# An expert layer's weights loaded in 8 KB runs, with its down product in high and low parts

## The chip, the cores and the metric

The kernel runs on one core of one Trainium2 chip. The time is that of one execution on the device, in microseconds (us). The reference's outputs have to be met within the tolerance of the problem.

## What is computed

The input is one sequence of 512 tokens of width 1024 (and 256 context tokens). A first block of layers (modulation, two scans, attention-free mixing, a feed-forward layer) is followed by two layers of a second block. Each of these ends in a mixture of experts, and only that is touched here. Cut to it, for one layer:

```python
# 32 experts, 2 of them for each of 512 tokens; w_gate, w_up [32, 1024, 256]; w_down [32, 256, 1024]
def expert_block(args):
    xe, e = args
    hid = jax.nn.silu(xe @ w_gate[e]) * (xe @ w_up[e])
    return hid @ w_down[e]
yb = lax.map(expert_block, (xb, block_expert)).reshape(-1, d)
```

The rows that come out are weighted by the router's probabilities and added up for each token. All is float32. The weights of one expert are three matrices of 1 MB, 201 MB over 32 experts and two layers.

## The kernel before, in words

The program is written by hand for each engine: every engine has its own list of instructions, and semaphores order them. All weights of the whole kernel pass through a ring of four slots in SBUF, `ring` (L101), 16 KB per partition each. `load` (L220) is what SyncE (SP) does for one chunk: it waits until the slot is free (`chunk_free`, counted up by TensorE behind its last use) and issues two DMAs, both on the slot's own semaphore; `landed` (L225) waits for both. A second name, `ring_r`, gives the same memory as float32r.

A float32 product on TensorE runs as one slow fp32 matmul or, in `mm3` (L174), as three matmuls of float32r operands: each operand is parted into a high part (its value rounded by ScalarE in a Copy to float32r) and a low part (the difference, by VectorE), and high x high, high x low and low x high are added.

In a layer's expert stage, an expert b has two chunks (`ex_up`, `ex_down`, L2190): gate and up weights (2 MB) and down weights (1 MB). In SP's queue they stand as up(0), up(1), down(0), up(2), down(1) and so on, and in the ring each chunk takes the slot of the fourth before it. The loads of gate and up (`gu_halves`, L2197) put row k x 128 + p on partition p, side by side: each partition gets eight runs of 256 floats (1 KB) per matrix. The down load (`dn_halves`, L2201) takes rows f x 128 + p, f = 0 and 1, with one DMA for each f: 128 partitions, a run of 4 KB in each.

Every expert is given a block of 80 token rows. GpSimd gathers them (L2519) with an indirect DMA from `x_rows` in DRAM into `xg`, one row per partition on partitions 0 to 79. Then, for expert b in `body`:

- TensorE (L2307): gate and up product `up(b)`, 24 matmuls in two halves h over k (L2261, in `mm3`, recorded at L178 to L180); turning of the next expert's gathered rows, eight blocks of 128 columns (L2258); down product of expert b - 1 (L2271, 4 fp32 matmuls, 8 records at L154); turning of the hidden rows of b, two blocks (L2268). Behind `up` and `down` it frees the slot.
- ScalarE (L2402): high part of the next expert's gate and up weights, half 0 (L2357), waiting first for their landing and for the half buffer; silu of b (L2360); high part of the turned rows (L2354); half 1; copy of the turned hidden rows (L2363); issue of the store of the output rows of b - 1 to `y_rows` in DRAM (L2366), from partitions 0 to 79.
- VectorE (L2483): low parts of the two halves (L2441), in place in the ring, each behind its high part; between them the product of silu and up (L2444) and the low part of the turned rows (L2438); last, the copy of the output rows of b - 1 out of PSUM (L2447).

`first` and `last` are the same steps for the first and the last expert; `overflow` code runs only where an expert has over 80 rows. After the experts, GpSimd gathers each token's two rows back from `y_rows` (L2548, 128 partitions) and TensorE weights and adds them.

The high parts have one buffer for each half: half h of the next expert waits until TensorE is through with half h of this one:

```python
def w_hi(b, n, it, h, first=False):
    if h == 0:
        landed(act, ex_up(n), R + it)
    if not first:
        act.wait_ge(S(("ex_wu", "ex_gu")[h]), b)
    weights_hi(ex_up(n), h).then_inc(S("ex_wh"), 1)
```

Of the kernel before, what the change touches and what calls it, by code (L numbers as in the profile page):

```python
# [57 lines left out]
def build(nc, t):  # L58
    with ExitStack() as ctx:
# [38 lines left out]
        def large(suffix, dt, held):  # L98
            return [held.enter_context(nc.sbuf_tensor(n + suffix, shape, dt)) for n, shape in (
                ("hT", [P, KD, LAT + CTX]),  # L100
                ("ring", [P, SLOTS, KD, HB]),  # L101
                ("arena", [P, ARENA]))]

        with ExitStack() as place:
            hT, ring, arena = large("", F32, place)
        hT_r, ring_r, arena_r = large("_parts", F32R, ctx)
# [61 lines left out]
        def slot(n):  # L168
            return ring[:, n % SLOTS, :, :]
# [22 lines left out]
        def unit_of(chunks, n, q):  # L192

            return chunks[:, n % SLOTS, 2 * q:2 * q + 2, :].rearrange("p k (c n) -> p (k c) n", n=CTX)

        def slot_lo(n):
            return ring_r[:, n % SLOTS, :, :]
# [101 lines left out]
        lent = ring[:, LENT % SLOTS, :, :].rearrange("p k n -> p (k n)")  # L299
# [830 lines left out]
        def down_rows(n):  # L1130

            return ring[:, n % SLOTS, 0:4, :].rearrange("p (f h) n -> p f (h n)", f=2)
# [9 lines left out]
        def down_unit(chunks, k):  # L1142
            return chunks[:, (N_DN + k // 2) % SLOTS, 2 * (k % 2):2 * (k % 2) + 2, :].rearrange("p k (c n) -> p (k c) n", n=CTX)
# [1107 lines left out]
        def half_of(chunks, n, h):  # L2251

            return chunks[:, n % SLOTS, 4 * h:4 * h + 4, :]

        def experts_pe(pe, lay, R):
            def turn_rows(c):
                for k in range(KD):
                    last = nc.tensor.transpose(ps[:, k // 4, (k % 4) * CAP:(k % 4 + 1) * CAP], xg[:, c, k * P:(k + 1) * P], ident[0:CAP, 0:CAP])  # L2258
                return last

            def gate_up(c, n, h):  # L2261

                return mm3(ps[0:CAP, 2 + c, :], [(xt_hi[:, c, 4 * h + k, :], xt_lo[:, c, 4 * h + k, :], ew_hi[:, h, k, :], slot_lo(n)[:, 4 * h + k, :])
# [525 lines left out]
```

## Time and profile before

| what | us |
|---|---|
| median of 3 runs | 3377.92 |
| lowest and highest | 3375.75, 3384.12 |
| profiled execution, first to last instruction (span) | 3394.1 |
| expert stage of layer 1, about | 1840 to 2208 |
| expert stage of layer 2, about | 2984 to 3348 |

The profile was taken of one execution; for it the page gives the span, and no other time. Times in its views are us from the start of the span, unless marked ns. PE is TensorE, PEld its weight loads, DVE VectorE, ACT ScalarE, POOL GpSimd, SP SyncE. A digit in a row of 40 slices is the busy share of one slice of 84.9 us in tenths. The DMA share is that of 16 DMA engines; it can stand a little over 1, as packets of several queues overlap. Queue q1 carries SP's loads, q10 ScalarE's transfers, q0 GpSimd's gathers. In brackets behind a row of the timeline stands the idle time of the engine before it and what ended it.

### The profile page before, as it was taken

To read this page: it belongs to the slowest core of one execution; us is meant where nothing else is said; L and a number is where in the kernel's file an instruction comes from. 1 tells how busy PE (TensorE), PEld (TensorE's weight loads), DVE (VectorE), ACT (ScalarE), POOL (GpSimd) and SP (SyncE) were. 2 spreads that over 40 slices of the span, in tenths; PEclk is the share of its full clock that TensorE was granted. 3 is DMA by queue.
4 is the path that set the end of the run, shared out by engine and by line. 5 is a ranking of instruction groups with operands and counts; after the bars stand their busy time and mean duration, and the time that the engine had idled before them with its cause. 6 is when DMAs were issued, how large, how long until landed. Compare 5 with 4: busy or idle time off the path is not lost. (4 is left out here: it accounts for less than half of the span.)

```text
span 3394.1 us, 31106 instructions
## 1 busy us (share of the span) xinstructions
PE 2851.6 (84%) x10872; PEld 1823.9 (54%) x10872; DVE 1410.1 (42%) x2118; ACT 1094.6 (32%) x1661; POOL 176.3 (5%) x202
## 2 busy tenths in 40 slices
PE   7899876679998698789986988857968999688995
PEld 1464455367876475367774444425734777544442
DVE  0104177332223155333344555524543333465554
ACT  1103322132223346432222444314373222144441
POOL 0000000000000000000001111100000000021210
PEclk9889988889999799799996999978987999699998
DMA  8301200122223111022223999921201112289994
GB/s 308 117 25 50 96 1 7 48 75 81 68 75 115 51 50 50 0 87 75 75 89 107 322 334 330 328 81 36 100 0 62 59 66 78 77 268 332 327 335 155
DMA packets 262715, 419.18 MB, mean 124 GB/s; under 512 B 17399, under 2 KB 179207, under 8 KB 262535
## 3 DMA queue, kind: packets, MB, share of 16 engines
q1 hardware_dynamic: 236448, 340.55, 30.3%
q10 hardware_dynamic: 17703, 47.76, 3.7%
q0 software_dynamic: 8448, 29.37, 3.0%
q8 instruction: 67, 1.10, 0.1%
q14 instruction: 49, 0.40, 0.0%
HBM read 390.37 MB, written 31.20 MB: 124 GB/s over the span
## 5 line engine op out<-in xcount | busy, mean ns | idle before, releaser
L178 PE MATMUL banks<-arena_parts,hT_parts 128*128 128x512 f32 x1056 | 439.0, 416 | 40.0 <-DVE ring_parts L208 28.4
L180 PE MATMUL banks<-arena_parts,ring_parts 128*128 128x512 f32 x1056 | 415.9, 394 | 0.0
L2441 DVE TENSOR_TENSOR ring_parts<-ring,hT_parts 128x2048 fp32r<-128x2048 f32 x128 | 292.5, 2286 | 294.8 <-ACT hT_parts L2357 294.7
L178 PE MATMUL banks<-hT_parts,arena_parts 128*80 128x512 f32 (+1 forms) x880 | 355.7, 404 | 42.2 <-DVE hT_parts L2438 18.2
L154 PE MATMUL banks<-ring,arena 128*80 128x512 f32 (+3 forms) x776 | 363.7, 615 | 15.1 <-DMA ring<-in_w_mod 10.9
L208 DVE TENSOR_TENSOR ring_parts<-ring,hT_parts 128x1024 fp32r<-128x1024 f32 x156 | 191.1, 1225 | 443.0 <-ACT hT_parts L204 440.3
L2357 ACT ACTIVATE hT_parts<-ring 128x2048 fp32r<-128x2048 f32 x128 | 243.9, 1907 | 355.4 <-DMA ring<-in_w_exp_up 336.6
L179 PE MATMUL banks<-ring_parts,arena_parts 128*80 128x512 f32 (+1 forms) x880 | 350.1, 398 | 0.0
L179 PE MATMUL banks<-hT_parts 128*128 128x512 f32 x864 | 338.7, 392 | 0.0
L204 ACT ACTIVATE hT_parts<-ring 128x1024 fp32r<-128x1024 f32 x156 | 165.1, 1058 | 503.0 <-PE banks L180 493.5
L154 PE MATMUL banks<-arena 128*128 128x512 f32 (+4 forms) x616 | 211.7, 486 | 62.1 <-DMA arena<-y_rows,arena 25.6
L178 PEld LDWEIGHTS banks<-arena_parts,hT_parts 128*128 128x128 f32 x1056 | 200.8, 190 | 109.5 <-issue 67.6
L154 PE MATMUL banks<-ring,hT 128*128 128x512 f32 (+3 forms) x672 | 255.3, 538 | 3.2 <-ACT hT L985 2.1
L180 PEld LDWEIGHTS banks<-arena_parts,ring_parts 128*128 128x128 f32 x1056 | 200.4, 190 | 43.8
L154 PEld LDWEIGHTS banks<-ring,arena 128*80 128x80 f32 (+2 forms) x776 | 107.1, 146 | 200.1 <-issue 181.4
L178 PEld LDWEIGHTS banks<-hT_parts,arena_parts 128*80 128x80 f32 (+1 forms) x880 | 147.1, 167 | 112.5 <-issue 55.2
L180 PE MATMUL banks<-hT_parts 128*80 128x512 f32 x512 | 204.4, 399 | 0.0
L154 PEld LDWEIGHTS banks<-ring,hT 128*128 128x128 f32 x672 | 127.5, 206 | 126.3 <-issue 123.1
L179 PEld LDWEIGHTS banks<-hT_parts 128*128 128x128 f32 x864 | 164.2, 190 | 43.4 <-issue 11.5
L154 PEld LDWEIGHTS banks<-arena 128*128 128x128 f32 (+2 forms) x616 | 109.4, 208 | 131.0 <-issue 58.8
L179 PEld LDWEIGHTS banks<-ring_parts,arena_parts 128*80 128x80 f32 (+1 forms) x880 | 147.3, 167 | 53.1 <-issue 2.8
L180 PE MATMUL banks<-hT_parts,arena_parts 128*128 128x512 f32 x368 | 144.6, 393 | 0.0
(428 smaller groups left out, 3364.9 us busy)
## 6 DMA issues: line engine op xcount, KB each, us to landing
ring<-in_w_exp_gate SPq DMA_DIRECT2D x64, 1024.0 KB, 6.7
ring<-in_w_exp_up SPq DMA_DIRECT2D x64, 1024.0 KB, 10.8
ring<-in_w_exp_down SPq DMA_DIRECT2D x128, 512.0 KB, 4.3
ring<-in_w_in SPq DMA_DIRECT2D x58, 1024.0 KB, 7.1
ring<-in_w_mod SPq DMA_DIRECT2D x24, 1024.0 KB, 8.4
y_rows<-arena ACTq DMA_DIRECT2D x64, 320.0 KB
ring<-in_w_gate SPq DMA_DIRECT2D x11, 1024.0 KB, 5.4
ring<-in_w_up SPq DMA_DIRECT2D x11, 1024.0 KB, 7.8
```

What stands on the lines that cost most here:

```text
L154: last = nc.tensor.matmul(out, l, r, start=(i == 0), stop=(i == len(pairs) - 1))
L178: nc.tensor.matmul(out, lh, rh, start=start and i == 0, stop=False)
L179: nc.tensor.matmul(out, lh, rl, start=False, stop=False)
L180: last = nc.tensor.matmul(out, ll, rh, start=False, stop=stop and i == len(terms) - 1)
L204: nc.scalar.activation(hi_unit(s[1]), unit_of(ring, n, q), ACT.Copy).then_inc(S("unit_hi"), 1)
L208: nc.vector.tensor_tensor(unit_of(ring_r, n, q), unit_of(ring, n, q), hi_unit(s[1]).bitcast(F32), ALU.subtract).then_inc(S("unit_lo"), 1)
L2357: return A_(ew_hi[:, h, :, :], half_of(ring, n, h), ACT.Copy)
L2441: return V.tensor_tensor(half_of(ring_r, n, h), half_of(ring, n, h), ew_hi[:, h, :, :].bitcast(F32), ALU.subtract)
```

## The change

1. The ring becomes four tensors, one for each slot, of the same size; the accesses are rewritten for it.
2. Gate and up weights: partition p takes rows 8p to 8p + 7 of each matrix, 8 KB that lie together in DRAM and, in a slot, together too. Gate fills the first half of a slot and up the second; one DMA for each, over 128 partitions.
3. So that row and weight agree, the gathered rows are turned by every eighth column: block k has columns k, k + 8, k + 16 and so on.
4. Down weights: partition p takes rows 2p and 2p + 1, 8 KB; one DMA for partitions 0 to 63 and one for 64 to 127. The hidden rows are turned by every second column.
5. The down product becomes three float32r matmuls for each fp32 one (12 in place of 4). ScalarE makes the high part of the down weights (128 x 2048) at the start of an expert's step, for the expert before; VectorE makes the low part right behind it, in place; the turned hidden rows get a low part as well.
6. The copy of the output rows out of PSUM moves from VectorE to ScalarE, in front of its copy of the hidden rows.
7. TensorE's down product waits for the low part of the down weights (`ex_dl`) in place of their landing; ScalarE now waits for the landing.

The diff, cut to its core (the same is done to the overflow code, and `ring[:, n % SLOTS, ...]` is rewritten everywhere):

```diff
-                ("ring", [P, SLOTS, KD, HB]),
-                ("arena", [P, ARENA]))]
+                ("arena", [P, ARENA]),
+                *((f"ring{i}", [P, KD, HB]) for i in range(SLOTS)))]
...
-        ew_hi = hT_all_r[:, 0:4096].rearrange("p (h k n) -> p h k n", h=2, k=4)
+        ew_hi = hT_all_r[:, 0:4096].rearrange("p (h a k n) -> p h a k n", h=2, a=2, k=4)
...
-        e_ht = A(12040, 2, 2, CAP)
+        ht_hi = A_r(12040, 2, 2, CAP)
+        ht_lo = A_r(11720, 2, 2, CAP)
+        dn_hi = A_r(0, 2, D)
...
+        def gu_rows(chunks, n):
+
+            return chunks[n % SLOTS][:, :, :].rearrange("p (a k) (c n) -> p a (k c) n", a=2, n=EF)
+
         def gu_halves(n, wg, wu):
-            return [(slot(n)[:, :, 0:EF], wg.rearrange("a (k p) n -> p (a k) n", p=P)),
-                    (slot(n)[:, :, EF:2 * EF], wu.rearrange("a (k p) n -> p (a k) n", p=P))]
+            return [(gu_rows(ring, n)[:, a], w.rearrange("a (p k) n -> p (a k) n", p=P)) for a, w in enumerate((wg, wu))]
+
+        def dn_rows(chunks, n):
+            return chunks[n % SLOTS][:, 0:4, :].rearrange("p (f h) n -> p f (h n)", f=2)
 
         def dn_halves(n, wd):
-            v = wd.rearrange("a (f p) n -> p (a f) n", p=P)
-            return [(down_rows(n)[:, f, :], v[:, f, :]) for f in range(2)]
+            v = wd.rearrange("a (p f) n -> p (a f) n", p=P)
+            h = P // 2
+            return [(dn_rows(ring, n)[h * i:h * (i + 1)], v[h * i:h * (i + 1)]) for i in range(2)]
...
-                    last = nc.tensor.transpose(ps[:, k // 4, (k % 4) * CAP:(k % 4 + 1) * CAP], xg[:, c, k * P:(k + 1) * P], ident[0:CAP, 0:CAP])
+                    last = nc.tensor.transpose(ps[:, k // 4, (k % 4) * CAP:(k % 4 + 1) * CAP], xg[:, c, k::KD], ident[0:CAP, 0:CAP])
...
-                    last = nc.tensor.transpose(ps[:, 6, f * CAP:(f + 1) * CAP], e_h[:, c, f * P:(f + 1) * P], ident[0:CAP, 0:CAP])
+                    last = nc.tensor.transpose(ps[:, 6, f * CAP:(f + 1) * CAP], e_h[:, c, f::2], ident[0:CAP, 0:CAP])
...
-            def rows_out(c, w):
+            def rows_out(c, n):
+                w = dn_rows(ring_r, n)
                 for h in range(2):
-                    last = mm(ps[0:CAP, 4 + h, :], [(e_ht[:, c, f, :], w[:, f, h * HB:(h + 1) * HB]) for f in range(2)])
+                    cols_ = slice(h * HB, (h + 1) * HB)
+                    last = mm3(ps[0:CAP, 4 + h, :], [(ht_hi[:, c, f, :], ht_lo[:, c, f, :], dn_hi[:, f, cols_], w[:, f, cols_]) for f in range(2)], True, True)
                 return last
...
-            def down(b, c, n, it):
-                j, r = ex_down(n), R + it
-                landed(pe, j, r)
+            def down(b, c, n):
+                pe.wait_ge(S("ex_dl"), b + 1)
                 pe.wait_ge(S("ex_ht"), b + 1)
                 pe.wait_ge(S("ex_yb"), b + 1)
-                rows_out(c, down_rows(j)).then_inc(S("ex_dn"), 1)
+                rows_out(c, ex_down(n)).then_inc(S("ex_dn"), 1)
                 pe.drain().then_inc(S("chunk_free"), 1)
...
+            def d_hi(b, n, it):
+                landed(act, ex_down(n), R + it)
+                down_hi(ex_down(n)).then_inc(S("ex_dh"), 1)
...
             def body(b, c, n, it):
+                d_hi(b - 1, n - 1, it)
                 w_hi(b + 1, n + 1, it, 0)
                 silu(b, c)
                 x_hi(b + 1, 1 - c)
                 w_hi(b + 1, n + 1, it, 1)
+                rows(b - 1, 1 - c, n - 1, it)
                 copy_h(b, c)
                 store(b - 1, 1 - c)
...
             def body(b, c, n, it):
+                d_lo(b - 1, n - 1)
                 w_lo(b + 1, n + 1, 0)
                 mult(b, c)
                 x_lo(b + 1, 1 - c)
                 w_lo(b + 1, n + 1, 1)
-                rows(b - 1, 1 - c, n - 1, it)
+                h_lo(b, c)
```

`down_hi` and `down_lo` are one ScalarE Copy of 128 x 2048 into `dn_hi` and one VectorE subtraction of the same size; `h_lo` is a VectorE subtraction of 128 x 160.

## Rows read from the trace of the kernel before

**Rows 1.** The page: busy time, and DMA and GB/s in 40 slices.
```profile
PE 2851.6 (84%) x10872; PEld 1823.9 (54%) x10872; DVE 1410.1 (42%) x2118; ACT 1094.6 (32%) x1661; POOL 176.3 (5%) x202
...
DMA  8301200122223111022223999921201112289994
GB/s 308 117 25 50 96 1 7 48 75 81 68 75 115 51 50 50 0 87 75 75 89 107 322 334 330 328 81 36 100 0 62 59 66 78 77 268 332 327 335 155
```

**Rows 2.** Windows of the first expert stage: start:end, us, busy us by engine, PEclk, DMA share, GB/s.
```profile
1880.00:2180.00 300.00, 271.36 (x1100) 140.48 (x1099) 174.03 (x130) 128.17 (x131) 53.05 (x50) 0.99 1.02 332
```

**Rows 3.** Line 2268 by source, in each layer: ns min/median/max, first and last start.
```profile
L2268 PE MATMUL banks<-ident,arena x64: 232/258/289, 1840.3 to 2195.5; 80*128 80x80 f32 x64
...
L2268 PE MATMUL banks<-ident,arena x64: 232/258/289, 2983.5 to 3337.0; 80*128 80x80 f32 x64
```

**Rows 4.** Who waited for whom, 1880 to 2180 us: total us, times, longest.
```profile
ACT hT_parts L2357 <- DMA ring<-in_w_exp_up: 156.7, 27, 7.7
DVE ring_parts L2441 <- ACT hT_parts L2357: 124.4, 26, 6.7
```

**Rows 5.** Timeline of one expert: start us, us, engine, line, operation.
```profile
2004.08 0.45 PE L178 MATMUL banks<-hT_parts,arena_parts 128*80 128x512 f32 x1 [0.47 <-DVE hT_parts L2438]
...
2009.46 0.39 PE L180 MATMUL banks<-hT_parts 128*80 128x512 f32 x1
2009.79 1.91 ACT L2357 ACTIVATE hT_parts<-ring 128x2048 fp32r<-128x2048 f32 x1 [5.84 <-DMA ring<-in_w_exp_up]
...
2010.14 0.77 PE L2258 MATMUL banks<-ident,arena 80*128 80x80 f32 x8 [0.30 <-issue]
...
2010.75 3.60 PE L154 MATMUL banks<-ring,arena 128*80 128x512 f32 x8
...
2014.45 0.35 PE L2268 MATMUL banks<-ident,arena 80*128 80x80 f32 x2
...
2015.22 0.46 PE L178 MATMUL banks<-hT_parts,arena_parts 128*80 128x512 f32 x1 [0.41 <-DVE hT_parts L2438]
```

**Rows 6.** DMA queues, 1880 to 2180 us: packets, MB, share of 16 engines.
```profile
q1 hardware_dynamic: 61927, 82.82, 84.8%
q0 software_dynamic: 2400, 8.19, 10.4%
q10 hardware_dynamic: 2502, 8.55, 7.1%
```

**Rows 7.** Windows: 1 KB weights; 4 KB weights; beside a gather; last store of a layer alone.
```profile
1873.00:1876.00 3.00, 2.11 (x7) 0.53 (x5) 3.00 (x3) 2.59 (x3) 0.44 (x1) 1.00 1.06 361
1880.50:1882.50 2.00, 1.89 (x10) 1.01 (x9) 0.00 (x0) 0.69 (x1) 0.00 (x0) 1.00 1.05 407
1890.50:1892.50 2.00, 2.00 (x11) 1.25 (x10) 0.00 (x0) 0.00 (x0) 0.00 (x0) 1.00 1.01 242
...
3344.00:3345.00 1.00, 0.00 (x0) 0.00 (x0) 0.00 (x0) 0.54 (x1) 0.00 (x0) 1.00 0.96 266
```

**Rows 8.** DMA queues, 1890.5 to 1892.5 us: packets, MB, share.
```profile
q1 hardware_dynamic: 81, 0.29, 59.3%
```

**Rows 9.** Groups by line, 1880 to 2180 us, then one of the whole span.
```profile
L2441 DVE TENSOR_TENSOR ring_parts<-ring,hT_parts 128x2048 fp32r<-128x2048 f32 x52 | 118.9, 2286 | 124.5 <-ACT hT_parts L2357 124.4
L2357 ACT ACTIVATE hT_parts<-ring 128x2048 fp32r<-128x2048 f32 x53 | 101.1, 1907 | 156.7 <-DMA ring<-in_w_exp_up 156.7
...
L2447 DVE COPY arena<-banks 80x1024 f32<-80x1024 f32 x26 | 31.5, 1213 | 0.0
...
L2354 ACT ACTIVATE arena_parts<-banks 128x640 fp32r<-128x640 f32 x26 | 17.9, 689 | 1.5 <-PE banks L2258 1.5
L2258 PEld LDWEIGHTS banks<-ident,arena 80*128 80x128 f32 x208 | 16.0, 140 | 17.4 <-issue 17.4
...
L2363 ACT ACTIVATE arena<-banks 128x160 f32<-128x160 f32 x26 | 7.9, 303 | 17.3 <-PE banks L2268 17.3
...
L154 PEld LDWEIGHTS banks<-arena,hT 128*128 128x128 f32 x128 | 28.2, 332 | 0.1
```

More of the change, by code:

```diff
@@ L2309, in body @@
                 turn_x(1 - c, n + 1, it)
-                down(b - 1, 1 - c, n - 1, it)
+                down(b - 1, 1 - c, n - 1)
                 turn_h(b, c)
@@ L2315, in last @@
                 up(b, 1, b)
-                down(b - 1, 0, b - 1, 0)
+                down(b - 1, 0, b - 1)
                 turn_h(b, 1)
-                down(b, 1, b, 0)
+                down(b, 1, b)
             def overflow_pe():
@@ L2356, in weights_hi, with down_hi @@
             def weights_hi(n, h):
[L2357 removed]
+                return A_(ew_hi[:, h].rearrange("p a k n -> p a (k n)"), half_of(ring, n, h), ACT.Copy)
+            def down_hi(n):
+                return A_(dn_hi, dn_rows(ring, n), ACT.Copy)
             def silu_gate(c):
@@ L2385, in copy_h, with rows @@
                 act.wait_ge(S("ex_th"), b + 1)
-                hidden_turned(c).then_inc(S("ex_ht"), 1)
+                hidden_turned(c).then_inc(S("ex_hh"), 1)
+            def d_hi(b, n, it):
+                landed(act, ex_down(n), R + it)
+                down_hi(ex_down(n)).then_inc(S("ex_dh"), 1)
+            def rows(b, c, n, it):
+                act.wait_ge(S("ex_dn"), b + 1)
+                if n >= 2 or not isinstance(it, int):
+                    act.wait_ge(S(f"yb_out{c}"), 16 * ((n + 2) // 2) + 16 * it)
+                copy_rows(c).then_inc(S("ex_yb"), 1)
             def store(b, c):
@@ L2392, in first @@
             def first():
+                act.sem_inc(S("ex_yb"), 1)
+                for c in range(2):
+                    act.sem_inc(S(f"yb_out{c}"), 16)
                 x_hi(0, 0)
@@ L2411, in last @@
                 b = NE - 1
+                d_hi(b - 1, b - 1, 0)
                 silu(b, 1)
+                rows(b - 1, 0, b - 1, 0)
+                d_hi(b, b, 0)
                 copy_h(b, 1)
                 store(b - 1, 0)
+                rows(b, 1, b, 0)
                 store(b, 1)
@@ L2419, in experts_act @@
                 act.sem_inc(S("ov_xt"), 1)
+                act.sem_inc(S("ov_yb"), 1)
+                act.sem_inc(S("ov_out"), 16)
+                act.wait_ge(S("yb_out0"), 16 * (NE // 2 + 1))
                 with act.Fori(0, OVER, 1) as k:
@@ L2459, in mult, with d_lo, h_lo @@
                 hidden(c).then_inc(S("ex_hid"), 1)
-            def rows(b, c, n, it):
-                dve.wait_ge(S("ex_dn"), b + 1)
-                if n >= 2 or not isinstance(it, int):
-                    dve.wait_ge(S(f"yb_out{c}"), 16 * ((n + 2) // 2) + 16 * it)
-                copy_rows(c).then_inc(S("ex_yb"), 1)
+            def d_lo(b, n):
+                dve.wait_ge(S("ex_dh"), b + 1)
+                down_lo(ex_down(n)).then_inc(S("ex_dl"), 1)
+            def h_lo(b, c):
+                dve.wait_ge(S("ex_hh"), b + 1)
+                hidden_lo(c).then_inc(S("ex_ht"), 1)
             def first():
-                dve.sem_inc(S("ex_yb"), 1)
-                for c in range(2):
-                    dve.sem_inc(S(f"yb_out{c}"), 16)
                 x_lo(0, 0)
@@ L2487, in body @@
                 w_lo(b + 1, n + 1, 1)
-                rows(b - 1, 1 - c, n - 1, it)
+                h_lo(b, c)
             def last():
                 b = NE - 1
+                d_lo(b - 1, b - 1)
                 mult(b, 1)
-                rows(b - 1, 0, b - 1, 0)
-                rows(b, 1, b, 0)
+                d_lo(b, b)
+                h_lo(b, 1)
             steps(dve, body, first, last)
             with overflows(dve):
-                dve.sem_inc(S("ov_yb"), 1)
-                dve.sem_inc(S("ov_out"), 16)
-                dve.wait_ge(S("yb_out0"), 16 * (NE // 2 + 1))
                 with dve.Fori(0, OVER, 1) as k:
```

51 lines of the change are left out of this document (31 added, 20 removed).

## Prediction

> **What bounds the kernel now.** I read the page first: TensorE is busy 84% of the span, but the DMA row is at 9 in two stretches only, late in the span, where the GB/s row stands at 322 to 335 [rows 1]. These are the two expert stages, 32 experts in each of two layers, and the change touches nothing that costs time outside them. The table of windows then says what is full there: in 300 us DMA is busy at 1.02 of its 16 engines and TensorE for 271 us at full clock, while VectorE works 174 us and ScalarE 128 us [rows 2]. So two resources are near their limit. The first and last turning of the hidden rows give the period of one expert: (2195.5 - 1840.3)/31 = 11.46 us and (3337.0 - 2983.5)/31 = 11.40 us, 11.43 us in the mean [rows 3]. There are 2 x 31 = 62 such periods; a change of 0.1 us in one is 6 us in the kernel.
>
> The waits tell which of the two limits ends last: ScalarE stands 156.7 us of these 300 waiting for the landing of w_exp_up, and VectorE stands behind ScalarE [rows 4]. The timeline shows TensorE's own floor, in an expert where it hardly waits: gate and up product from 2004.08, turning of the next rows at 2010.14, down product 2010.75 to 2014.35, turning of the hidden rows at 2014.45, next gate and up product at 2015.22: 11.14 us [rows 5]. DMA therefore sets the period, with TensorE only 0.3 us behind. Any gain must lower both.
>
> **Part 1, the DMA bill.** The queue rows of these 300 us give prices with all their contention in: weights 82.82 MB in 84.8% of 300 us = 254 us, or 326 GB/s; gathered rows 8.19 MB in 31.2 us, 262 GB/s; stores 8.55 MB in 21.3 us, 401 GB/s [rows 6]. Per expert: 3.146 MB of weights 9.66 us, 0.328 MB gathered 1.25 us, 0.328 MB stored 0.82 us, sum 11.73 us; over the share of 1.02 that is 11.5 us, the period measured.
>
> *Longer runs.* Gate and up weights now come in runs of 1 KB. A stretch with these alone moves 361 GB/s, a stretch with 4 KB runs (down weights) 407 GB/s [rows 7]. Per engine a 1 KB run takes 1024/22.6 = 45.4 ns and a 4 KB run 4096/25.4 = 161 ns: 38.6 ns per KB and 6.8 ns per run. 8 KB then takes 316 ns, 415 GB/s (an estimate from these two rows). Gate and up, 2.097 MB: 5.81 us before, 5.05 us after, -0.76 us. Bounds: nothing, and -1.1 us if the contention shrinks in proportion. The down weights would go from 2.58 us to 2.53 us by the run length alone.
>
> *Half the partitions.* But the down weights are also cut differently: before, two DMAs of 128 partitions each; after, one of partitions 0 to 63 and one of 64 to 127, behind one another in SP's queue. The trace has transfers that touch 80 partitions. The last store of a layer runs alone and all its engines are busy (0.96), yet it moves 266 GB/s; and where a gather to 80 partitions is in flight the whole core falls to 242 GB/s at share 1.01, the weights' own packets with it (0.29 MB in 59.3% of 2 us, 245 GB/s) [rows 7, 8]. Transfers over 128 partitions give 361 to 407. Engines are as busy and move less: they queue for the part of SBUF that 80 partitions reach. In proportion, 80/128 of 407 is 254, which is what is measured; 64/128 gives 203 GB/s. So the down weights cost 2.58 us with no such limit (lower end), 1.049/0.254 = 4.13 us at the rate of the 80-partition rows, and 5.17 us at 203 GB/s (upper end). I take 4.13 us, since the 16 engines are not in step and some write the second half while others write the first: +1.55 us. Of this I take back 0.25 us, a third of the store's 0.82 us, since stores read SBUF and can go while writes stall. The sum: -0.76 + 1.55 - 0.25 = +0.54 us per expert, period 12.0 us.
>
> The Trainium skill, "SBUF — State Buffer", section "Door 1: The DMA port swizzle", says that partitions 0 to 63 reach only 8 of 16 ports (196 GB/s against 328 for 128 partitions), and its section on hitting both halves with two DMAs gives just 6% over a single one. By it the down weights would take 1.049/0.208 = 5.0 us, an estimate from that page, and the kernel would come out near the upper end. The trace agrees for 80 partitions; no run yet shows 64.
>
> **Part 2, TensorE.** The down product falls from 4 fp32 products, 3.60 us, to 12 of the other kind at (2009.46 - 2004.08)/23 = 0.234 us, 2.81 us [rows 5]: -0.79 us, floor 10.35 us. While DMA sets the period this is worth nothing; if DMA gets out of the way, it decides. The turned rows are read at every eighth column. The eight loads stand in 0.54 us (2010.14 to 2010.68), each 140 ns long; the trace has no strided load that I can name, so the bounds are nothing and 8 x (332 - 140) = 1.5 us, by the slowest load of 128 columns [rows 9]. I take nothing: the same number of elements. Cover: DMA, up to 12.0 us; without it the floor is 10.35 to 11.9 us.
>
> **Part 3, ScalarE and VectorE.** ScalarE gains the high part of the down weights, one instruction of 2048 columns, 1.91 us, and the row copy: from 160 columns at 303 ns and 640 at 689 ns, 1024 columns take 1.00 us [rows 9]. 128.17/26.2 experts = 4.9 us becomes 7.8 us per expert. VectorE loses the copy (1.21 us) and gains the low part (2.29 us) and that of the hidden rows (at most 0.3 us): 6.6 becomes 8.0 us [rows 2, 9]. Both fit in 10.35 us, so the cost is nothing if the order allows it. **The new waits:** ScalarE begins an expert by waiting for the down weights of the one before. Behind it stand the next expert's high part, the silu and the turned rows; but these weights are ahead of the next expert's in SP's queue, and ScalarE waits for the latter until 5.7 us after the product's start (2004.08 to 2009.79), so 1.91 us is idle time of today [rows 5]. TensorE waits for the low part, ready some 4.5 us after its gate and up product starts, where it wants it at 6.7 us. The row copy holds up ScalarE's copy of the hidden rows by 1 us; only the down product one expert later reads that. The cover of all this is the 5 us that ScalarE waits for DMA per expert; if DMA lands early, the cover is TensorE's 10.35 us. The queues of SP and POOL have the same DMAs, with the same slots; four tensors for one moves nothing. At a layer's end the last down product saves 0.8 us, twice, and the added low part of the hidden rows takes 0.3 back: -1 us.
>
> **Sum.** 62 x 0.54 - 1 = +33 us. The profiled span is 3394.1 us, 16 us over the median of 3377.92 us, and no time of the profiled execution itself is given beside the span; I put the difference on the median, 3411 us.
>
> **Rivals.** (a) *The halves cost little and it gets faster.* Engines that lag by half a microsecond write different halves, and stretches with 128 partitions at 4 KB show 407. Then DMA is 11.73 - 0.76 - 0.05 = 10.92, over 1.02 10.7 us, above TensorE's 10.35: -0.73 x 62 - 1 = -46, 3332 us; at TensorE's floor -68, 3310 us. For it: weights are packed in one queue without gaps, so lags persist. Against: the lone store, and weights slowed beside a gather. It wins wherever the down weights take under 3.3 us. (b) *Half and half:* down weights at about 3.4 us, a change under 10 us, 3378 us. (c) *The strided loads bind:* TensorE's floor at 11.9 us, +0.3 us as today, 12.2 us: +48, 3425 us. The skill speaks for it in "Advanced Engine Details and Errata", section "Memory Cachelines": SBUF lines are 16 bytes, and a different line for every access costs; eight fp32 columns are 32 bytes. No row here shows it. (d) *The runs do not become 8 KB*, as their view still has eight rows of 1 KB: then -0.76 falls away, +1.3 x 62 - 1 = +80, 3458 us; nothing but the order of the view speaks for it.
>
> **How the numbers follow.** Forecast 0.44; (a) 0.38; (b) 0.10; (c) 0.05; (d) 0.03. Under 0.3% (10 us) a measurement can't tell from no change. Faster 0.39, same 0.10, slower 0.51. The forecast's own range is 3390 to 3465 (down weights at 3.7 to 5 us); that of the whole is 3318 to 3460, which leaves out the full 203 GB/s and TensorE's bare floor.
>
> **What would show it.** After: packets under 2 KB fall by some 130,000; expert stretches at share 1.0 but near 300 GB/s; rates near 200 to 250 GB/s in the 4 us of each pair of down loads; ScalarE still waiting for w_exp_up; period 12.0 us. Wrong would be: rates over 350 there and TensorE waiting for nothing (a); turning of eight blocks over 1 us (c).

## Result, and the profile after

| kernel | median us | runs | profiled execution, us | span, us |
|---|---|---|---|---|
| before | 3376.84 | 4 | | 3394.1 |
| after | 3468.39 | 4 | 3475.85 | 3474.1 |

The ratio of the times is 1.0244, with a 95% interval of 1.0208 to 1.028: the changed kernel is 2.4% slower, 82 us of 3377 (the medians of the table lie 92 us apart; the working below goes by ratios). The profiled execution is the slowest of the four, so single readings of its trace can lie somewhat above those of a typical one. Forecast were 3411 us, with a range up to 3460. The sign was right; the size was far off, and outside the range.

The page of after, the rows that answer to [rows 1] and the count of DMA packets:

```profile
PE 2888.4 (83%) x11128; PEld 1908.4 (55%) x11128; DVE 1499.9 (43%) x2182; ACT 1272.6 (37%) x1789; POOL 189.7 (5%) x202
...
DMA  8311200112122120022127999711102222399994
GB/s 303 112 46 51 70 1 28 49 59 87 61 81 94 49 73 25 10 100 73 73 75 217 322 322 325 255 50 44 54 0 85 73 73 87 120 304 275 287 276 138
DMA packets 139836, 419.19 MB, mean 121 GB/s; under 512 B 17399, under 2 KB 48135, under 8 KB 115079
```

The first expert stage moves 322 to 325 GB/s, a little less than before. The second moves only 275 to 304 where it moved 327 to 335, with the same 9 in the DMA row. The page of before counts 179207 packets under 2 KB, so they fell by 131072: the long runs are really there.

Windows of after: start:end, us, busy us by engine, PEclk, DMA share, GB/s. First the stage of layer 1, 2 us in which the halves of a pair of down loads are in flight, and two stretches with gate and up weights; then, from the stage of layer 2, the whole and three stretches:

```profile
1900.00:2200.00 300.00, 271.20 (x1194) 169.97 (x1192) 208.00 (x154) 197.05 (x180) 63.09 (x48) 0.97 1.02 322
1903.00:1905.00 2.00, 2.00 (x10) 1.28 (x9) 1.94 (x1) 0.00 (x0) 0.00 (x0) 1.00 1.02 223
1910.00:1912.00 2.00, 1.65 (x8) 1.08 (x9) 2.00 (x2) 1.58 (x3) 0.33 (x1) 1.00 0.99 418
1921.00:1924.00 3.00, 2.83 (x13) 1.85 (x13) 1.83 (x2) 2.23 (x3) 0.00 (x0) 1.00 1.00 415
...
3050.00:3400.00 350.00, 292.93 (x1223) 182.23 (x1222) 212.44 (x158) 201.78 (x186) 59.84 (x50) 0.91 0.97 286
...
3050.00:3085.00 35.00, 31.04 (x137) 19.45 (x136) 23.21 (x19) 22.88 (x21) 9.42 (x6) 0.96 1.03 322
3120.00:3155.00 35.00, 25.86 (x99) 15.81 (x98) 18.55 (x14) 17.13 (x17) 5.52 (x5) 0.79 0.98 260
3295.00:3330.00 35.00, 25.32 (x98) 15.34 (x97) 20.59 (x16) 20.59 (x20) 3.15 (x5) 0.83 0.91 265
```

Both prices of DMA can be read: 415 and 418 GB/s for runs of 8 KB, as worked out, and 223 GB/s at share 1.02 where the halves run, between the forecast's 203 and 254. All 16 engines are as busy, and half as much moves. In layer 2 the granted clock falls too, to 0.79 in one stretch; the kernel before has 0.99 there (3000 to 3340 us).

The turning of the hidden rows by source, one answer for each layer (ns min/median/max, first and last start), gives the period as [rows 3] did:

```profile
L2277 PE MATMUL banks<-ident,arena x64: 281/339/408, 1848.7 to 2211.4; 80*128 80x80 f32 x64
...
L2277 PE MATMUL banks<-ident,arena x64: 281/342/409, 3008.9 to 3410.9; 80*128 80x80 f32 x64
```

(2211.4 - 1848.7)/31 = 11.70 us in layer 1 and (3410.9 - 3008.9)/31 = 12.97 us in layer 2, where before had 11.46 and 11.40. The forecast was 12.0 for both. The stages lost 7.5 + 48.5 us of the 80 us of span. The other 24 us were lost outside them, where the forecast had nothing: layer 1's first turning already starts 8.4 us later than before.

DMA queues of after, 1900 to 2200 us (packets, MB, share of 16 engines), beside [rows 6]:

```profile
q1 hardware_dynamic: 11401, 80.00, 82.1%
q0 software_dynamic: 2400, 8.19, 10.8%
q10 hardware_dynamic: 2496, 8.52, 8.8%
```

Weights now take 246.3 us for 80.00 MB, 325 GB/s, where they had 326. Long runs and halves cancel. Stores fell from 401 to 8.52/(0.088 x 300) = 323 GB/s: they have become dearer.

Waits, 1900 to 2200 us, total us, times, longest:

```profile
ACT hT_parts L2368 <- DMA ring<-in_w_exp_up: 81.5, 26, 4.5
DVE ring_parts L2484 <- ACT hT_parts L2368: 73.1, 28, 4.1
```

The chain of [rows 4] is there still: ScalarE waits for the landing of w_exp_up. Its total is smaller mainly because ScalarE has more work (197 us for 128).

Groups by line, 1900 to 2200 us, for the added and moved operations, and the timeline of one expert on TensorE:

```profile
L2487 DVE TENSOR_TENSOR ring_parts<-ring,arena_parts 128x2048 fp32r<-128x2048 f32 x26 | 59.6, 2293 | 18.9 <-ACT arena_parts L2371 18.9
L2371 ACT ACTIVATE arena_parts<-ring 128x2048 fp32r<-128x2048 f32 x26 | 49.8, 1917 | 15.6 <-issue 10.3 <-DMA ring<-in_w_exp_down 5.3
...
L2380 ACT ACTIVATE arena<-banks 80x1024 f32<-80x1024 f32 x25 | 25.4, 1016 | 2.4 <-PE banks L180 2.4
L2267 PEld LDWEIGHTS banks<-ident,arena 80*128 80x128 f32 x208 | 25.1, 203 | 17.5 <-issue 17.5
...
L2491 DVE TENSOR_TENSOR arena_parts<-banks,arena_parts 128x160 fp32r<-128x160 f32 x26 | 8.1, 313 | 0.0
```

```profile
1998.14 1.11 PE L2267 MATMUL banks<-ident,arena 80*128 80x80 f32 x8 [0.30 <-issue]
1999.05 0.44 PE L178 MATMUL banks<-arena_parts 128*80 128x512 f32 x1
...
2001.64 0.39 PE L180 MATMUL banks<-arena_parts 128*80 128x512 f32 x1
2002.86 0.46 PE L2277 MATMUL banks<-ident,arena 80*128 80x80 f32 x2 [0.83 <-DVE arena L2494]
2003.68 0.45 PE L178 MATMUL banks<-hT_parts,arena_parts 128*80 128x512 f32 x1 [0.35 <-DVE hT_parts L2481]
```

Each priced instruction costs within 0.02 us what was forecast (1917, 2293, 1016 and 313 ns). One that was priced at nothing does not: the load of a turned block takes 203 ns instead of 140 ns, and eight blocks stand 1.11 us where they stood 0.77 us [rows 5]. The twelve matmuls of the down product start (2001.64 - 1999.05)/11 = 0.235 us apart, 2.8 us in all, as worked out.

### The profile page after: what moved, and what is told of

Same layout as the page of the kernel before. It is cut to its first block and busy times, and to the rows that moved or that the text cites. A ratio compares the mean times of both kernels' runs of the same rounds, so it can differ in the third digit from the quotient of the medians.

```text
span 3474.1 us, 31822 instructions
## 1 busy us (share of the span) xinstructions
PE 2888.4 (83%) x11128; PEld 1908.4 (55%) x11128; DVE 1499.9 (43%) x2182; ACT 1272.6 (37%) x1789; POOL 189.7 (5%) x202
## 3 DMA queue, kind: packets, MB, share of 16 engines
q8 instruction: 68, 1.11, 0.1%
## 5 line engine op out<-in xcount | busy, mean ns | idle before, releaser
L179 PE MATMUL banks<-ring_parts,arena_parts 128*80 128x512 f32 (+1 forms) x1136 | 468.2, 412 | 0.0
L180 PE MATMUL banks<-arena_parts,ring_parts 128*128 128x512 f32 x1056 | 419.3, 397 | 0.0
L178 PE MATMUL banks<-hT_parts,arena_parts 128*80 128x512 f32 (+1 forms) x880 | 374.1, 425 | 39.5 <-DVE hT_parts L2481 16.0
L179 PEld LDWEIGHTS banks<-ring_parts,arena_parts 128*80 128x80 f32 (+1 forms) x1136 | 194.0, 171 | 75.8 <-issue 13.0
L180 PEld LDWEIGHTS banks<-arena_parts,ring_parts 128*128 128x128 f32 x1056 | 200.4, 190 | 47.6
L178 PEld LDWEIGHTS banks<-hT_parts,arena_parts 128*80 128x80 f32 (+1 forms) x880 | 154.3, 175 | 117.1 <-issue 62.4
L180 PE MATMUL banks<-hT_parts 128*80 128x512 f32 x512 | 217.4, 425 | 0.0
L179 PEld LDWEIGHTS banks<-hT_parts 128*128 128x128 f32 x864 | 164.1, 190 | 47.1 <-issue 11.5
L2487 DVE TENSOR_TENSOR ring_parts<-ring,arena_parts 128x2048 fp32r<-128x2048 f32 x64 | 146.7, 2292 | 52.8 <-ACT arena_parts L2371 52.8
L180 PE MATMUL banks<-hT_parts,arena_parts 128*128 128x512 f32 x368 | 146.8, 399 | 0.0
L154 PE MATMUL banks<-ring,arena 128*2 128x512 f32 (+2 forms) x264 | 125.1, 623 | 13.6 <-DMA ring<-in_w_mod 12.0
## 6 DMA issues: line engine op xcount, KB each, us to landing
ring<-in_w_exp_up SPq DMA_DIRECT2D x64, 1024.0 KB, 11.5
ring<-in_w_exp_down SPq DMA_DIRECT2D x128, 512.0 KB, 10.9
```

Source lines behind the costliest of these rows:

```text
L154: last = nc.tensor.matmul(out, l, r, start=(i == 0), stop=(i == len(pairs) - 1))
L178: nc.tensor.matmul(out, lh, rh, start=start and i == 0, stop=False)
L179: nc.tensor.matmul(out, lh, rl, start=False, stop=False)
L180: last = nc.tensor.matmul(out, ll, rh, start=False, stop=stop and i == len(terms) - 1)
L2487: return V.tensor_tensor(dn_rows(ring_r, n), dn_rows(ring, n), dn_hi.bitcast(F32), ALU.subtract)
```

## Experiments

The theory after the result: the halves of the down weights slow DMA. Rivals: the strided turning, the new waits, the number or the order of the DMAs, and the ring in four tensors, which also moved behind the arena. "Of before" is always against runs of the kernel before taken on the same chip alongside (3386.08, 3389.48 and 3382.87 us in the median). Executions of one kernel spread over some 30 to 40 us, so parts of the time are compared by ratios. A period is the mean of one layer of one profiled execution; the profiled execution can be the fastest or the slowest of its kernel, and that is said where it matters.

### The halves

**down_full**: the changed kernel, with the down weights in two DMAs over 128 partitions each. The runs are 4 KB then.

```diff
-            h = P // 2
-            return [(dn_rows(ring, n)[h * i:h * (i + 1)], v[h * i:h * (i + 1)]) for i in range(2)]
+            return [(dn_rows(ring, n)[:, f, :], v[:, f, :]) for f in range(2)]
```

> The changed kernel with its down weights loaded over 128 partitions again, two DMAs of 4 KB runs. Theory H (the halves are the cost): down weights 2.6 us in place of 5 us, so an expert takes about 10.9 us in both layers, TensorE stays at full clock, and the kernel comes to 3350 to 3375 us, level with the kernel before or a little below. Theory T (TensorE is the cost: turned rows read with a stride at 0.111 us a block where it was 0.069, matmuls 2 to 3% slower): over 3430 us, little better than the 3468 us of the changed kernel. Theory W (the new waits on ScalarE and VectorE are the cost): also over 3430 us.

Measured: 3388.9 us, 1.0024 of before [0.9998, 1.0051]; periods 10.8 and 11.2 us. Most of the loss is gone with this one line, 2.2 of 2.4%, so without the halves the rest of the change about breaks even. The time is above what was expected, so something else costs some 20 us.

**before_halves**: the kernel before, and only the down weights in halves (the hidden rows turned by every second column to match).

```diff
-            v = wd.rearrange("a (f p) n -> p (a f) n", p=P)
-            return [(down_rows(n)[:, f, :], v[:, f, :]) for f in range(2)]
+            v = wd.rearrange("a (p f) n -> p (a f) n", p=P)
+            h = P // 2
+            return [(down_rows(n)[h * i:h * (i + 1)], v[h * i:h * (i + 1)]) for i in range(2)]
...
-... e_h[:, c, f * P:(f + 1) * P] ...
+... e_h[:, c, f::2] ...
```

> The kernel before with one edit: the down weights in two DMAs of 64 partitions each, 8 KB runs (and the hidden rows turned by every second column, as that needs). Theory H: down weights go from 2.6 to 5 us, nothing is won at gate and up, so an expert takes 12.9 to 13.8 us and the kernel 3470 to 3520 us, no better than the changed kernel. Theories T and W: 3370 to 3385 us, no change.

Measured: 3553.52 us, 1.0542 [1.0486, 1.0599]; periods 13.8 and 13.4 us (in the profiled execution, the fastest of four). The halves alone cost more here (5.4%) than the whole change does, and more than expected. The window and the weights' queue row, 1880 to 2180 us:

```profile
1880.00:2180.00 300.00, 244.74 (x917) 127.67 (x916) 144.38 (x109) 107.12 (x110) 25.45 (x44) 0.94 1.03 279
```

```profile
q1 hardware_dynamic: 49406, 69.34, 87.2%
```

Share 1.03 and 279 GB/s, for 1.02 and 332 in [rows 2]. The weights move at 69.34/261.6 = 265 GB/s: 3.146 MB take 11.87 us, 2.2 us more than the 9.66 of before. That is what 64 partitions at the 223 GB/s of the window would add, 1.049/0.223 - 2.58 = 2.1 us.

**down_mid**: the changed kernel, the down weights in three DMAs: partitions 32 to 95, then 0 to 31 and 96 to 127, the third with a semaphore of its own for which ScalarE waits too.

```diff
+        def dn_three(n, wd):
+            v = wd.rearrange("a (p f) n -> p (a f) n", p=P)
+            return [(dn_rows(ring, n)[i:j], v[i:j]) for i, j in ((32, 96), (0, 32), (96, 128))]
```

> The changed kernel with its down weights in three DMAs: partitions 32 to 95, then 0 to 31, then 96 to 127, all 8 KB runs. Theory P (it matters which partitions a transfer touches: 0 to 63 share one half of the ways into SBUF, 64 to 127 the other): partitions 32 to 95 go at full speed, 1.3 us for 0.5 MB, the other two at half speed, 2.5 us together: 3.8 us in place of 5, about -1 us for an expert, kernel 3390 to 3420 us. Rival N (it matters how many partitions a transfer touches): 64 at 203 GB/s and 32 at about 100 GB/s, 2.6 + 5.2 = 7.8 us, kernel over 3550 us.

Measured: 3409.8 us, 1.0101 [1.0055, 1.0147]; periods 11.5 and 11.0 us. Window 1880 to 2180 us:

```profile
1880.00:2180.00 300.00, 269.49 (x1192) 168.95 (x1190) 210.49 (x156) 198.37 (x182) 67.03 (x51) 0.97 0.99 328
```

**gu_only**: the kernel before, and only gate and up weights in 8 KB runs, with the gathered rows turned by every eighth column; down weights and down product as before.

```diff
-            return [(slot(n)[:, :, 0:EF], wg.rearrange("a (k p) n -> p (a k) n", p=P)),
-                    (slot(n)[:, :, EF:2 * EF], wu.rearrange("a (k p) n -> p (a k) n", p=P))]
+            return [(gu_rows(ring, n)[:, a], w.rearrange("a (p k) n -> p (a k) n", p=P)) for a, w in enumerate((wg, wu))]
...
-... xg[:, c, k * P:(k + 1) * P] ...
+... xg[:, c, k::KD] ...
```

> The kernel before with only gate and up weights in 8 KB runs and the gathered rows turned by every eighth column; the down product stays fp32 and its loads stay as before, the ring too. Theory F: TensorE's floor is 11.14 + 0.34 = 11.5 us, so the faster transfers are worth nothing: an expert takes 11.5 to 11.7 us, the kernel 3385 to 3405 us, no faster than before. It also tells what the down product in high and low parts is worth, once the halves are gone. Rival D: 10.7 to 11 us an expert, the kernel 3340 to 3360 us.

Measured: 3369.57 us, 0.9956 [0.9929, 0.9984]; period 11.3 us in both layers; time and period lie between the two expectations. Weights move at 83.39/(0.781 x 300) = 356 GB/s, 8.84 us per expert: -0.82 us for the runs, where -0.76 was forecast. But only 0.16 us of that reaches the period, since TensorE is next (share 0.96, TensorE busy 283 of 300 us).

**gu_halves**: gu_only with the down weights in halves; the transfers of the changed kernel, the products of the kernel before. The edits to `dn_halves` and to the turning of the hidden rows are those of before_halves.

> gu_only with the down weights in two DMAs of 64 partitions: all of the changed kernel's transfers, with the ring, the down product and the engines' order of the kernel before. Theory B (with the halves in, DMA alone sets the period, and the rest of the change is hidden): as after_aligned, 3425 to 3450 us, 12.0 to 12.5 us an expert. Rival C (the halves cost more where the TensorE part of an expert is longer, since before_halves lost 167 us and the changed kernel only some 80 us against down_full): 3500 us or more.

Measured: 3473.0 us, 1.0267 [1.0216, 1.0319]; periods 12.5 and 13.1 us. ScalarE's wait, 1880 to 2180 us:

```profile
ACT hT_parts L2361 <- DMA ring<-in_w_exp_up: 168.2, 23, 8.7
```

The transfers alone cost as much as the whole change (the intervals overlap); with the ring's address put right (after_aligned below, 1.0136) the rest of the change saves 1.3% beside them. The result lies between what the two theories expected, so the price of the halves is no constant. (The first two pairs also have the hidden rows turned by every second column, 0.08 us per expert at most.)

| kernel without the halves | ratio | with them | ratio | halves cost |
|---|---|---|---|---|
| before | 1 | before_halves | 1.0542 | 5.4%, 183 us |
| gu_only | 0.9956 | gu_halves | 1.0267 | 3.1%, 105 us |
| down_full | 1.0024 | after | 1.0244 | 2.2%, 74 us |
| full_aligned (below) | 0.9955 | after_aligned (below) | 1.0136 | 1.8%, 61 us |

### The ring's address

**ring_split**: the kernel before, with only the ring as four tensors behind the arena (part 1 of the change).

```diff
-                ("ring", [P, SLOTS, KD, HB]),
-                ("arena", [P, ARENA]))]
+                ("arena", [P, ARENA]),
+                *((f"ring{i}", [P, KD, HB]) for i in range(SLOTS)))]
```

> The kernel before with one edit: the ring as four tensors behind the arena. In the changed kernel the matmuls in three parts follow each other by 0.231 to 0.236 us where it was 0.227, also in stages that the change doesn't touch (the feed-forward of the first block, the gates). Theory L (the place of the operands in SBUF does that): the same here, +15 to +22 us, 3392 to 3400 us, all of it outside the expert stages. Rival (the chip or the day does it): within 5 us of the kernel before, and 0.227 us.

Measured: 3405.47 us, 1.0082 [1.0048, 1.0116]; periods 11.5 and 11.4 us, as before. So the split costs 0.8%, and not in the expert stages. In a long product of the first block the matmuls come more slowly. A window of 30 us there, before and after:

```profile
735.00:765.00 30.00, 29.55 (x131) 24.16 (x130) 7.52 (x8) 6.39 (x7) 0.00 (x0) 1.00 0.41 132
```

```profile
735.00:765.00 30.00, 29.55 (x127) 23.48 (x127) 7.50 (x7) 6.39 (x7) 0.00 (x0) 1.00 0.37 118
```

131 matmuls became 127 at full clock: 0.229 and 0.236 us each. ring_split has 127 there too. Counted in bytes of a partition from the start of hT, the ring began behind hT's 24576, a multiple of 128; behind hT and the arena's 25000 x 4 bytes it begins at 124576, 32 bytes past one.

**split_aligned**: ring_split, and the arena 96 bytes longer.

```diff
-ARENA = 25000
+ARENA = 25024
```

> The kernel before with the ring in four tensors behind the arena (as ring_split) and the arena 24 columns longer. Theory A: as the kernel before, 3380 to 3392 us, matmuls 0.227 us apart. Rival S: as ring_split, +0.8%, 3405 us.

Measured: 3386.0 us, 1.0002 [0.9977, 1.0027], and 131 matmuls in the window. The four tensors cost nothing; the 32 bytes do. (The small tensors behind the ring move by 96 bytes as well, but in the kernel before they stand where they stand in ring_split.) The window shows it in every kernel: 130 or 131 matmuls wherever the ring starts at a multiple of 128, 127 or 128 in ring_split, after, down_full and down_mid. Which multiple counts (32 past 128 is also 32 past 64) was not tested.

How the start address does it stays open. In this window the ring is only loaded as weights, by every third matmul (L180); the moving operands lie in hT and the arena and start at multiples of 128 in both kernels. The mean distance of matmuls in all such groups of three is 226.9 ns in split_aligned and 233.4 in ring_split. In the first block's down product and others like it the ring is the moving operand of every third matmul, and the distance goes from 227.3 to 232.0 ns; in the experts' gate and up product it is that too, and the distance is 233.0 and 233.8 ns. So the same 32 bytes cost 3%, 2% and next to nothing.

**full_aligned**: down_full with the same longer arena.

> The changed kernel with down weights over 128 partitions (as down_full) and the arena 24 columns longer, so that the ring's slots start at multiples of 128 bytes in a partition (100096 + 24576), where they start 32 bytes past one (100000 + 24576). Theory A (the start address of the ring makes the matmuls in three parts slower): they follow each other by 0.227 us again, and the kernel is 15 to 20 us faster than down_full, 3360 to 3375 us, 0.3 to 0.7% faster than the kernel before. Rival S (it is the split into four tensors or the order itself): as down_full, 3385 to 3395 us.

Measured: 3366.98 us, 0.9955 [0.9926, 0.9984]; 131 matmuls, periods 10.6 and 10.9 us. This beats down_full by 0.7% and the kernel before by 0.45%.

**after_aligned**: the changed kernel, with the longer arena and nothing else.

> The changed kernel with nothing but the arena 24 columns longer, so that the ring's slots start at multiples of 128 bytes. Theory A: the 0.8% of ring_split goes away here too: 1.6% slower than the kernel before in place of 2.4%, 3430 to 3445 us beside 3386 us. Rival (in the changed kernel DMA hides that): as the changed kernel, 2.4%.

Measured: 3432.39 us, 1.0136 [1.0084, 1.0187]; periods 11.9 and 12.4 us. So 1.1 of the 2.4% are the address. The two windows have to be read together with the DMA queues (packets, MB, share) of 1880 to 2180 us, full_aligned first, then after_aligned:

```profile
1880.00:2180.00 300.00, 269.94 (x1222) 170.05 (x1222) 214.16 (x159) 207.36 (x188) 85.94 (x52) 0.97 0.97 348
```

```profile
q1 hardware_dynamic: 19405, 86.64, 79.5%
q0 software_dynamic: 2509, 8.58, 9.5%
q10 hardware_dynamic: 2714, 9.22, 7.7%
```

```profile
1880.00:2180.00 300.00, 263.17 (x1152) 164.83 (x1151) 201.47 (x151) 190.48 (x175) 56.68 (x49) 0.96 1.00 316
```

```profile
q1 hardware_dynamic: 11197, 78.59, 79.7%
q10 hardware_dynamic: 2400, 8.19, 10.2%
q0 software_dynamic: 2340, 8.01, 10.2%
```

Per expert, halves out and in: weights 363 and 329 GB/s, 8.66 and 9.57 us; gather 301 and 262 GB/s, 1.09 and 1.25 us; store 399 and 268 GB/s, 0.82 and 1.22 us. The sum goes from 10.57 to 12.04 us, and a quarter of the difference is the store. This pair overstates it: the profiled execution of full_aligned is the fastest of its twelve (3350.31 us), that of after_aligned the slowest of its four (3452.03 us). The other pairs, 1880 to 2180 us, agree on the store but less strongly (before to before_halves 401 to 343 GB/s, gu_only to gu_halves 381 to 341), and not on the gather (262 to 266, 273 to 265).

### The turning

**unit_turns**: full_aligned, with the rows turned in blocks of neighbouring columns, as before the change. The weight rows do not match them then, so this kernel does not compute the reference's result; instructions and sizes are the same.

```diff
-... xg[:, c, k::KD] ...
+... xg[:, c, k * P:(k + 1) * P] ...
...
-... e_h[:, c, f::2] ...
+... e_h[:, c, f * P:(f + 1) * P] ...
```

> full_aligned with the gathered rows and the hidden rows turned by blocks of adjacent columns, as in the kernel before. The turned columns then don't belong to the weights they meet: the product of each expert is left wrong, all instructions and sizes stay. Theory F (with the halves gone TensorE's floor sets the period, so what turning costs is on the path): turning falls from 0.111 to 0.069 us a block, 10 blocks an expert, 0.42 us, 62 periods: 20 to 26 us faster than full_aligned. Rival D (DMA still sets the period): under 8 us.

Measured: 3345.01 us, 0.9876 [0.9829, 0.9923]; 22 us less than full_aligned, as expected. The loads by source, before_halves (every second column), full_aligned (every second), unit_turns:

```profile
L2269 PEld LDWEIGHTS banks<-ident,arena x128: 194/205/219, 1838.3 to 3465.4; 80*128 80x128 f32 x128
```

```profile
L2276 PEld LDWEIGHTS banks<-ident,arena x128: 194/205/219, 1828.6 to 3285.3; 80*128 80x128 f32 x128
```

```profile
L2276 PEld LDWEIGHTS banks<-ident,arena x128: 137/141/225, 1835.4 to 3291.3; 80*128 80x128 f32 x128
```

Every second column costs what every eighth does (203 ns on average for L2267 above).

**perm_once**: full_aligned, but the columns are put in order before they are turned. ScalarE permutes each token row once per layer, before it goes to `x_rows`, and VectorE writes the hidden rows permuted; all turning is of neighbouring columns, and the reference's result is computed.

```diff
-                act.dma_start(x_rows[i * P:(i + 1) * P, :], x_res[:, i, :]).then_inc(S("rows_out"), 16)
+                A_(x_perm[:, i, :].rearrange("p (k n) -> p k n", k=KD), x_res[:, i, :].rearrange("p (n k) -> p k n", k=KD), ACT.Copy).then_inc(S("x_permed"), 1)
...
+                act.dma_start(x_rows[i * P:(i + 1) * P, :], x_perm[:, i, :]).then_inc(S("rows_out"), 16)
```

> full_aligned with the strided turning taken away in another place: ScalarE writes the 512 token rows into a scratch with their columns already in the order 8p + k, once a layer, four copies of 1024 columns, and the gather fetches those; VectorE writes the hidden rows in the order that the down weights want. All turning then reads adjacent columns. Theory F: as unit_turns, some 22 us less than full_aligned, less 2 x 4 x 1 to 2 us for the copies, of which part is hidden: 3348 to 3358 us, 0.8 to 1.1% faster than the kernel before. Rival: the copies stand on the path of the router and strided writes are slow, so that nothing is left: 3362 to 3370 us.

Measured: 3346.24 us, 0.9899 [0.9855, 0.9942]; periods 10.5 and 10.8 us. Of the kernels that compute the reference's result this is the fastest: 1.0% faster than before and 3.4% faster than the changed kernel.

### The place of the row copy

**rows_dve**: full_aligned, with the copy of the output rows back on VectorE, in front of the low part of the hidden rows (and, for the last expert, the store ahead of the high part of the down weights).

```diff
-                rows(b - 1, 1 - c, n - 1, it)
                 copy_h(b, c)
...
                 w_lo(b + 1, n + 1, 1)
+                rows(b - 1, 1 - c, n - 1, it)
                 h_lo(b, c)
```

> full_aligned with the copy of the output rows on VectorE again, behind the low part of half 1, as in the kernel before (at the end of the layer the last store and the last high part change places, as the buffer needs). By the prediction's bill the place of this copy costs nothing on either engine: within 6 us of full_aligned, 3361 to 3373 us. Rival W (the order on ScalarE or VectorE is on the path): over 10 us off, in either direction.

Measured: 3421.97 us, 1.012 [1.0072, 1.0169]; periods 11.7 and 11.7 us. A clear miss: 55 us slower, where a few were expected. Waits, 1880 to 2180 us, and the timeline of one expert:

```profile
ACT arena_parts L2370 <- DVE arena L2500: 80.3, 26, 4.1
DVE ring_parts L2474 <- ACT arena_parts L2370: 64.2, 26, 2.7
...
PEld banks L178 <- DVE ring_parts L2474: 21.5, 20, 1.4
```

```profile
1999.08 1.21 DVE L2500 COPY arena<-banks 80x1024 f32<-80x1024 f32 x1
...
2000.48 0.32 ACTq L2382 DMA_DIRECT2D y_rows<-arena  x1
...
2001.27 1.92 ACT L2370 ACTIVATE arena_parts<-ring 128x2048 fp32r<-128x2048 f32 x1 [3.61 <-DVE arena L2500]
...
2003.22 2.29 DVE L2474 TENSOR_TENSOR ring_parts<-ring,arena_parts 128x2048 fp32r<-128x2048 f32 x1 [2.69 <-ACT arena_parts L2370]
...
2005.56 0.45 PE L178 MATMUL banks<-arena_parts 128*80 128x512 f32 x1 [0.87 <-DVE ring_parts L2474]
```

ScalarE ends an expert by issuing the store, which waits for the copy (L2500). VectorE comes to that copy only behind the low parts of the weights, 2.28 us each. Behind the store's wait on ScalarE stands the next high part of the down weights (L2370), idle for 3.61 us; behind that VectorE's low part, and behind that the down product. With the copy on ScalarE the store waits only for ScalarE's own work just ahead of it. So part 6 of the change is worth its place once the down product is in parts. That it is this wait is read from the timeline; issuing the store from another engine, which would test it, was not tried.

## Why the prediction was wrong, by its own steps

The ratios give a sum that can be laid beside the forecast's. Each line is the difference of two kernels, of 3382 us:

| step | forecast, us | measured, us | from |
|---|---|---|---|
| long runs, parts, copies; unit turning, aligned, no halves | -48 | -42 | unit_turns, 0.9876 |
| strided turning | 0 | +27 | full_aligned 0.9955 less unit_turns |
| down weights in halves, with the stores' relief | +81 | +61 | after_aligned 1.0136 less full_aligned |
| ring as four tensors, behind the arena | 0 | +36 | after 1.0244 less after_aligned |
| sum | +33 | +82 | |

(-48 is 62 x (-0.76) - 1, +81 is 62 x (1.55 - 0.25). Each measured line is uncertain by some 15 to 20 us, and a medians' difference in place of the ratios' gives 22 us for the turning and 36 again for the address. The sizes also hang on the order in which the steps are taken: the address costs 28 us in ring_split and 23 between down_full and full_aligned.)

**The failed step is "four tensors for one moves nothing".** It looked at the queues and slots alone. But the tensors stand in another order in the diff, which also put the ring 32 bytes past a multiple of 128, and products of the first block that read the ring pay for it: 3% per matmul in the window shown, 36 us in all where nothing was forecast. The same omission made the sentence "the change touches nothing that costs time outside them" wrong: 24 of the 80 us of span were lost there. The longer distances of matmuls add up to some 18 us (an estimate: 3 x 705 x 6.5 ns + 3 x 330 x 4.7 ns, from the groups of three above); where the rest goes is not shown. This is the larger of the two terms that were missing; the turning is the other.

**The strided turning "I take nothing" was wrong.** Its bounds were right (0 to 1.5 us). Eight blocks cost 1.11 for 0.77 us, +0.34 us, and two hidden blocks 0.08 us more. The forecast's cover, DMA up to 12.0 us, is thin: TensorE's own time stands beside DMA's, and 22 to 27 us show where the halves are out of the way. Rival (c) priced the floor too high, but named the right step. The rule it cited, of the Trainium skill's "Advanced Engine Details and Errata", "Memory Cachelines", asks for two hits on a 16-byte line; every second fp32 column has two, and pays in full (205 ns for 140). Here the measurement decides: that rule does not describe these loads.

**The halves were the right cause, with a price 20 us too high in the sum.** 223 GB/s was measured where 4.13 us stood for 254; at that rate the down weights take 4.7 us, an estimate from 2 us of trace, halfway to the upper end. In the changed kernel part of that is hidden, in before none (+2.2 us of weights per expert). Wrong was the relief of 0.25 us for stores: after's stores fell from 401 to 323 GB/s, +0.2 us. Beside the halves stores get dearer in every pair, and not freer. That the sum still came out on the right side is the halves' doing; that it was not off by more is luck, since 20 us too much here made up for a part of the 63 us missing above.

**The runs were right:** 415 GB/s forecast, 415 and 418 measured, and -0.82 us for -0.76. That the gain would stop at TensorE was said of rival (a); gu_only shows it (0.16 of 0.82 us).

**TensorE, ScalarE and VectorE:** the down product takes 2.8 us, ScalarE 1.92 + 1.02 us more, VectorE 2.29 + 0.31 us more, as forecast. The floor of 11.14 us was no bare floor: perm_once runs at 10.5 us and not at 10.35, and single periods of before lie on both sides of it (10.2 to 13.1 us). The new waits were not tested by themselves; with them in, unit_turns lands 6 us from the forecast, within the uncertainty. rows_dve shows that the copy's move to ScalarE was worth 55 us in this order, where the text had priced its place at nothing as long as the sums fit.

**The period** was near in layer 1, 11.70 us for 12.0, in part by luck, since the halves cost less and the turning more than was said. It was wrong in layer 2, 12.97. There stretches with a clock of 0.79 to 0.83 and 260 to 265 GB/s stand among others at up to 322 GB/s. A loop can be read into it: TensorE waits for weights, its clock falls, it frees slots late, and DMA idles. It was not tested. gu_halves, with the ring in its old place, has 13.1 us there after 12.5 in layer 1, so the address is not needed for it; before_halves has 13.8 and then 13.4, so the halves alone do not always make the second layer the slower one.

**Two small sums** of the forecast do not come out as written. With the relief of 0.25 us in, down weights at 3.4 us (rival (b)) give -13 us and not under 10, and at 3.7 us 3384 us and not 3390. Neither bears on the miss.

**What stays open:** why the same halves cost 183, 105, 74 and 61 us in four kernels. How far the 16 engines are out of step, and how much slack TensorE's own time leaves, were not separated. Whether halves issued from two queues would overlap was not tried.

## What to carry to other kernels

When a diff moves a tensor, work out its new start address, and compare the cadence of matmuls in a stage that the change does not touch: four matmuls fewer in 30 us were 1% of this kernel. Cut a large load so that each DMA reaches all partitions, or at least both halves; longer runs gain 0.8 us of DMA time per expert (0.16 of it reached the period in gu_only), and half the partitions take up to 2.2 away. Before a copy is moved between engines, look at what stands behind the wait for it: moved back alone, this one costs 55 us.

## What the runs showed of the hardware

- With a tensor that starts 32 bytes past a multiple of 128, in a long product that loads weights from it for every third float32r matmul of 512 columns, a matmul comes every 0.236 us and not every 0.229 (30 us over 127 and 131 matmuls). Where it is the moving operand, the cost was 2% in one product and next to nothing in another (227.3 to 232.0 ns, 233.0 to 233.8 ns; split_aligned and ring_split).
- A TensorE load of 80 x 128 fp32 takes 140 ns with neighbouring columns, and 203 to 205 ns both with every second and with every eighth.
- Beside loads to 64 partitions, stores from 80 partitions slow down as well, in all pairs of kernels: 401 to 343 GB/s (before and before_halves), 381 to 341 (gu_only and gu_halves), 399 to 268 (full_aligned and after_aligned). Gathers do so only in some.
- Engines at share 1.0 can mean 279 or 332 GB/s: a busy DMA row is no proof that bytes are moving at the full rate.
